# FoX attention by pairs of heads, with projections handed out in steps of three matmuls

## The reference

```python
q = rms_norm(q.reshape(b, t, FOX_HEADS, HEAD_DIM), q_norm)
k = rms_norm(k.reshape(b, t, FOX_HEADS, HEAD_DIM), k_norm)
cum_log_f = jnp.cumsum(jax.nn.log_sigmoid(f_logit), axis=1)
for start in range(0, t, FOX_BLOCK):          # FOX_BLOCK = 128
    end = start + FOX_BLOCK
    logits = jnp.einsum('bqhd,bkhd->bhqk', q[:, start:end], k[:, :end]) * scale
    logits = logits + cum_log_f[:, :, start:end, None] - cum_log_f[:, :, None, :end]
    probs = jax.nn.softmax(jnp.where(causal, logits, MASK_VALUE), axis=-1)
    outs.append(jnp.einsum('bhqk,bkhd->bqhd', probs, v[:, :end]))
o = rms_norm(jnp.concatenate(outs, axis=1), o_norm)
```

## Time and profile before

| | us |
|---|---|
| median of 3 runs | 1870.01 (1867.45 to 1887.97) |
| the profiled execution | 1867.99 |
| its span, first to last instruction | 1866.2 |
| TensorE matmul busy | 1731.4 (93%) |
| VectorE busy | 889.6 (48%) |
| ScalarE busy | 676.2 (36%) |

### The profile page before, as it was taken

One profiled execution on the slowest core, in us unless ns is written; L12 is line 12 of the kernel. 1 busy time (PEld: TensorE's weight loads), 2 busy tenths in 40 slices (PEclk: granted clock), 3 DMA queues, 4 the chain that ended last, 5 costly groups with the idle time before them and its releaser, 6 DMA issues.

```text
span 1866.2 us, 20863 instructions
## 1 busy us (share of the span) xinstructions
PE 1731.4 (93%) x8076; PEld 1374.7 (74%) x8076; DVE 889.6 (48%) x1487; ACT 676.2 (36%) x1218; POOL 74.2 (4%) x119
## 2 busy tenths in 40 slices
PE   6999998988888769699999999999999999999997
PEld 5787665655567546587888888888888888888886
DVE  4315584453636656545334434555543355555332
ACT  5224103633452353634434322434432334344321
POOL 2000430000001002000000000000000000000000
PEclk8999998898999899899999999999999999999999
DMA  4122000000002021350001102333323333433232
GB/s 138 45 47 46 13 12 12 23 12 12 12 23 68 12 68 57 111 194 11 14 1 46 45 29 87 94 102 91 96 74 96 101 113 98 123 92 107 85 96 96
DMA packets 166922, 121.32 MB, mean 65 GB/s; under 512 B 23448, under 2 KB 140456, under 8 KB 166824
## 3 DMA queue, kind: packets, MB, share of 16 engines
q1 hardware_dynamic: 165496, 115.53, 20.8%
q10 hardware_dynamic: 1328, 4.46, 0.7%
HBM read 115.77 MB, written 4.19 MB: 64 GB/s over the span
## 4 chain that ended last, share of the span: by engine, by line
PE 57%; DVE 1%; ACT 0%; DMA 0%; issue 0%; DVEq 0%
PE tail_b L99 17%; PE tail_b L101 17%; PE tail_b L100 17%; PE tail_b L2065 2%; PE tail_b L2040 1%; PE tail_b L2029 0%; PE tail_b L2052 0%; PE tail_b L1977 0%; DVE tail_wl L1741 0%; DMA tail_wr<-in_w_out 0%; PE tail_b L2184 0%; PE tail_b L2100 0%; DVE tail_xs L1776 0%; ACT tail_xs L1576 0%; DVE XR L1904 0%
## 5 line engine op out<-in xcount | busy, mean ns | idle before, releaser
L1897 DVE TENSOR_TENSOR ff_wl<-ff_wr,ff_wh 128x512 fp32r<-128x512 f32 (+1 forms) x176 | 168.5, 958 | 329.9 <-ACT ff_wh L1684 329.9
L1684 ACT ACTIVATE ff_wh<-ff_wr 128x512 fp32r<-128x512 f32 (+1 forms) x176 | 148.7, 846 | 377.9 <-PE tail_b L101 377.9
L99 PE MATMUL tail_b<-HH,ff_wh 128*128 128x512 f32 x704 | 273.9, 389 | 0.0
L100 PE MATMUL tail_b<-HL,ff_wh 128*128 128x512 f32 x704 | 273.9, 389 | 0.0
L101 PE MATMUL tail_b<-HH,ff_wl 128*128 128x512 f32 x704 | 273.9, 389 | 0.0
L99 PE MATMUL mix_gb<-HH,mix_wh 128*128 128x512 f32 x432 | 178.3, 413 | 7.7 <-ACT slots L444 3.8
L100 PE MATMUL mix_gb<-HL,mix_wh 128*128 128x512 f32 x432 | 171.5, 397 | 0.0
L101 PE MATMUL mix_gb<-HH,mix_wl 128*128 128x512 f32 x432 | 170.8, 395 | 0.0
L99 PE MATMUL tail_b<-tail_wh,HH 128*128 128x512 f32 x384 | 153.9, 401 | 10.0 <-DVE tail_wl L1741 8.8
L100 PEld LDWEIGHTS tail_b<-HL,ff_wh 128*128 128x128 f32 x704 | 132.2, 188 | 27.7
L99 PEld LDWEIGHTS tail_b<-HH,ff_wh 128*128 128x128 f32 x704 | 132.2, 188 | 27.5
(11 more groups left out here) (311 smaller groups left out, 2661.7 us busy)
## 6 DMA issues: line engine op xcount, KB each, us to landing
ff_wr<-in_ffn_w_up SPq DMA_DIRECT2D x88, 512.0 KB, 3.7
ff_wr<-in_ffn_w_down SPq DMA_DIRECT2D x88, 256.0 KB, 2.8
mix_wr<-in_w_in SPq DMA_DIRECT2D x26, 512.0 KB, 3.7
mix_wr<-in_xa_wkv SPq DMA_DIRECT2D x16, 512.0 KB, 3.7
XR<-in_x SPq DMA_DIRECT2D x8, 512.0 KB, 6.4
tail_wr<-in_w_out SPq DMA_DIRECT2D x16, 256.0 KB, 5.2
XR<-in_x ACTq DMA_DIRECT2D x1, 4096.0 KB, 18.7
tail_wr<-in_xa_wq SPq DMA_DIRECT2D x16, 256.0 KB, 4.6
```

What stands on the lines that cost most here:

```text
L99: pe.matmul(out, hi_w, hi_x, start=first, stop=False)
L100: pe.matmul(out, hi_w, lo_x, start=False, stop=False)
L1684: act.activation(part(FWH[m % FPART], m), part(FWR[m % FRAW], m), ACT.Copy).then_inc(w_hi, 1)
L1897: dve.tensor_tensor(part(FWL[m % FPART], m), part(FWR[m % FRAW], m), part(FWH[m % FPART], m), ALU.subtract)\
```

## The change

The 32 units become 16 pairs (`PAIRS`): both heads of `hp` for one block of queries. On TensorE, `scores(u, c)` issues piece c of the one head and then of the other, which use rows 0 to 63 and 64 to 127 of the array. `outputs(u)` goes over the key blocks and issues the value product of both heads for each; they write columns 0 to 63 and 64 to 127. `SC` has four buffers instead of three, `PTS` four, `CB` four, and the running sums of the second pair of heads are made among pairs 1 to 4 of the first.

VectorE scales no probabilities. The unscaled exponentials are transposed and multiplied with V; VectorE takes the reciprocals of both sums (`rin`), TensorE spreads each over 64 partitions by a matmul of the reciprocal column, broadcast, with the identity, and VectorE copies the result to `INV` and multiplies the output with it (`fox_out`, which ScalarE had before).

The projections in FoX go by steps, one step being the three matmuls of one k (`fill`). `FOX_PRE` has 6, 6, 5, 5, 5, 5 steps instead of six times 8, and every pair has two steps ahead of its later transposes (`FOX_A`) and two ahead of its outputs (`FOX_B`). ScalarE and VectorE do the copies and weight parts for a half in the round or pair in which it begins (`begun`), VectorE one pair later among the pairs.

```diff
-_FX = spread(2 * S0, 2 * G0, [1] * 6 + [1 if n in (4, 9, 14, 20, 25, 30) else 0 for n in range(33)])
-FOX_PRE, FOX_UNIT = _FX[:6], _FX[6:]
+def in_two(spans):
+    return spans[0::2], spans[1::2]
+def begun(span):
+    return -(-span[0] // KT), -(-span[1] // KT)
+_FX = spread(2 * S0 * KT, 2 * G0 * KT, [6, 6, 5, 5, 5, 5] + [2, 2] * 16)
+FOX_PRE, (FOX_A, FOX_B) = _FX[:6], in_two(_FX[6:])
...
+        PAIRS = [(hp, i) for hp in range(2) for i in range(NT)]
+        PIECES = [(u, c, hh) for u, (hp, i) in enumerate(PAIRS) for c in range(i // 4 + 1) for hh in range(2)]
...
ScalarE
+            def probs_out(u, g):
+                i = PAIRS[u][1]
+                w = len(blocks(i, g)) * P
+                for hh in range(2):
+                    m = group_of[(u, g, hh)]
+                    act.wait_ge(E("p_tr"), m + 1)
+                    if u >= 1:
+                        act.wait_ge(E("av_mm"), u)
+                    act.activation(PTS[2 * g + hh][:, 0:w], M[3 + m % 2][:, 0:w], ACT.Copy).then_inc(E("p_ev"), 1)
+            for u, (hp, i) in enumerate(PAIRS):
                 for g in range(i // 4 + 1):
+                    probs_out(u, g)
+                for entry in CUM_AT(u):
+                    cum_out(entry)
+                new = range(*begun((FOX_A[u][0], FOX_B[u][1])))
+                for m in new:
+                    copy_out(m)
+                if u + 1 < len(PAIRS):
+                    fox_exp(u + 1)
+                for m in new:
+                    halves(m, m + 1)
...
VectorE
-            def probabilities(n):
-                sc, keys = SC[n % 3], (FOX_UNITS[n][1] + 1) * P
-                dve.wait_ge(E("expd"), n + 1)
-                link(dve.reciprocal(RIN[:, n:n + 1], SUM[:, n:n + 1]))
-                dve.tensor_scalar(sc[:, 0:keys], sc[:, 0:keys], RIN[:, n:n + 1], None, ALU.mult).then_inc(E("probs"), 1)
+            def inverse_sums(u):
+                dve.wait_ge(E("expd"), 2 * u + 2)
+                dve.reciprocal(RIN[:, 2 * u:2 * u + 2], SUM[:, 2 * u:2 * u + 2]).then_inc(E("rin"), 1)
+            def fox_out(u):
+                hp, i = PAIRS[u]
+                dve.wait_ge(E("av_mm"), u + 1)
+                dve.tensor_copy(INV[:], M[5][:, P:2 * P]).then_inc(E("inv"), 1)
+                dve.wait_ge(E("inv"), u + 1)
+                dve.tensor_tensor(MX[:, hp, i * P:(i + 1) * P], M[5][:, 0:P], INV[:], ALU.mult).then_inc(E("av_ev"), 1)
+            logits(0)
+            maxima(0)
+            late = range(0)
+            for u in range(len(PAIRS)):
+                if u:
+                    fox_out(u - 1)
+                if u + 1 < len(PAIRS):
+                    logits(u + 1)
+                inverse_sums(u)
+                if u + 1 < len(PAIRS):
+                    maxima(u + 1)
+                for m in late:
+                    halves(m, m + 1)
+                late = range(*begun((FOX_A[u][0], FOX_B[u][1])))
...
TensorE
+            def outputs(u):
+                hp, i = PAIRS[u]
+                if u:
+                    pe.wait_ge(E("av_ev"), u)
+                pe.wait_ge(E("rin"), u + 1)
+                for hh in range(2):
+                    n = 2 * u + hh
+                    pe.matmul(M[5][64 * hh:64 * hh + 64, P:2 * P], RIN[:, n:n + 1].to_broadcast([P, 64]), ident,
+                              start=True, stop=True, skip_group_check=True)
+                for g in range(i // 4 + 1):
+                    pe.wait_ge(E("p_ev"), group_of[(u, g, 1)] + 1)
+                    for k in blocks(i, g):
+                        for hh in range(2):
+                            mm = pe.matmul(M[5][64 * hh:64 * hh + 64, 0:P],
+                                           VT[:, k, 128 * hp + 64 * hh:128 * hp + 64 * hh + 64],
+                                           PTS[2 * g + hh][:, (k % 4) * P:(k % 4 + 1) * P], start=(k == 0), stop=(k == i),
+                                           skip_group_check=True)
+                mm.then_inc(E("av_mm"), 1)
+            for entry in CUM(0):
+                cum_row(entry)
+            scores(0, 0)
+            for u, (hp, i) in enumerate(PAIRS):
+                new = u + 1 < len(PAIRS)
+                if new:
+                    scores(u + 1, 0)
+                if u == 0:
+                    fill(*FOX_A[u])
+                transposes(u, 0)
+                if new and PAIRS[u + 1][1] >= 4:
+                    scores(u + 1, 1)
+                if u:
+                    fill(*FOX_A[u])
+                if i >= 4:
+                    transposes(u, 1)
+                for entry in CUM_AT(u):
+                    cum_row(entry)
+                fill(*FOX_B[u])
+                outputs(u)
+            pe.wait_ge(E("av_ev"), len(PAIRS))
             norms(12, 16)
```

More of the change, by code:

```diff
@@ L622, in _, with cum_out @@
[L622 to L632, removed]
+            def cum_out(entry):
+                _, h, v = entry
+                m = group_of[entry]
+                if h >= 2:
+                    act.wait_ge(E("gated"), 2)
+                act.wait_ge(E("p_tr"), m + 1)
+                act.activation(half(CB[h], v), M[3 + m % 2][:], ACT.Copy).then_inc(E("p_ev"), 1)
@@ new lines, in maxima @@
+            def maxima(u):
+                i = PAIRS[u][1]
+                keys = (i + 1) * P
+                for hh in range(2):
+                    n, sc = 2 * u + hh, SC[2 * (u % 2) + hh]
+                    dve.wait_ge(E("sc_read"), piece_of[(u, i // 4, hh)] + 1)
+                    link(dve.tensor_tensor(sc[:, keys - P:keys], sc[:, keys - P:keys], NEGQ[:], ALU.add))
+                    dve.tensor_reduce(NM[:, n:n + 1], sc[:, 0:keys], AX.X, ALU.max, negate=True).then_inc(E("neg_max"), 1)
@@ L1231, in _, with transposes @@
-            pe.wait_ge(E("n_out"), 12)
-            for n in range(33):
-                if n % 16 == 0 and n < 32:
-                    if n:
-                        outputs(n - 1)
-                    cum_rows(n // 16)
-                    scores(n)
-                    scores(n + 1)
-                    continue
-                if n < 32 and (n + 1) % 16:
-                    scores(n + 1)
-                halves(*FOX_UNIT[n])
-                outputs(n - 1)
+            def transposes(u, g):
+                i = PAIRS[u][1]
+                for hh in range(2):
+                    m = group_of[(u, g, hh)]
+                    pe.wait_ge(E("expd"), 2 * u + hh + 1)
+                    pe.wait_ge(E("p_ev"), m - 1)
+                    for k in blocks(i, g):
+                        last = pe.transpose(M3[3 + m % 2][:, k % 4, :], SC[2 * (u % 2) + hh][:, k * P:(k + 1) * P], ident)
+                    last.then_inc(E("p_tr"), 1)
```

165 lines of the change are left out of this document (64 added, 101 removed).

## The result

The changed kernel takes 1806.34 us (median of 4, 1803.33 to 1807.4), the one before beside it 1868.77 (1867.45 to 1887.97). The ratio is 0.9646, with a 95% interval of 0.959 to 0.9703. I had said 1814 and 1802 to 1832; the kernel is 8 us better than that. The profiled executions took 1867.99 and 1803.33 us, 64.7 apart, against 54.5 forecast: some 10 us have to be found in my terms. The profiled execution is the fastest of the four; the kernel's second profile (experiment 8) took 1807.5, and where the two differ is said there.

What follows compares the result with a forecast made beforehand. TensorE was taken to bound every pair; its stretch terms, 118.1 us, became 124.2 with waits, clock and last output, against 168.3. That 44.1 plus 10.4 from the rounds, 54.5, off 1867.99 gave 1813.5, said as 1814; range 1802 to 1832.

Steps and rivals of the forecast that it cites:

- Both overlaps: Attention stretch: two heads' scores run side by side, halving 30.7 us of stream; value products likewise, halving 31.4.
- no rival: Rivals included: chain sets the pace, 1831, chance 0.13; one alternation doesn't overlap, 1829, chance 0.10; both fail, 1845, chance 0.02.
- the chain sets the pace: Rival: value products through exponentials bound each pair; exponentials 2 us late make pairs wait 1.1, so 1831; chance 0.13.
- 0.3 for entering and leaving each of 16 groups: Value products in the attention stretch: group cost added to 15.7 us of stream, making 20.5 us.
- My lower bound: Whole time 1802: group costs 0.1 instead of 0.3 (8 less), clock and chain costing nothing (3.5 less).
- I take 2.5: Attention stretch: 2.5 us allowed for a short spell at 1.2 GHz, between 0 and 10.
- 2.2 + 1.0: TensorE's waits in the stretch: about 2.2 us at the start for VectorE's gates, 1.0 where TensorE doesn't bound a pair.
- The last output costs 0.4 more: End of the attention stretch: 0.4 us added, as VectorE scales the last output.
- It is 1.3 more on 144: Value products: 1.3 us more if only the SSD rate of 0.135 per matmul holds.
- The clock at 10 and the start's wait doubled: Case for the forecast's own upper bound: low clock costing 10 us and the start's wait doubled, 1826.
- the doubled drains: Case for the upper bound: TensorE's tiling-change price of 0.2 to 0.3 per group doubled, about 12 us more, 1826.
- 1.5 after the pair's start: Pair of eight key blocks: second exponential's transposes come 1.5 us into the next pair, so the chain's period is 7.95.

Runs made afterwards that it cites:

- experiment 8: Changed kernel with seven projection steps moved from pairs with slack to the last norms: 1798.25 us; the unedited changed kernel, rerun beside it, 1807.17 us.
- 3: Changed kernel with both heads' score matmuls reading the first head's rows, 0 to 63: 1820.06 us, stretch 14.7 us more.
- 2: Changed kernel with both heads' value products in columns 0 to 63 from the second pair on: 1826.3 us, stretch 15.3 us more.
- 4: Kernel before, units by single heads, with only the projections changed to steps of three matmuls: 1844.65 us against 1867.78 us beside it.
- 7: Changed kernel with each row maximum issued twice on VectorE: 1813.72 us, stretch 6.6 us more.
- 6: Changed kernel with VectorE scaling the probabilities by the sums again before the transposes, without the small matmuls: 1806.9 us against 1807.17 us unedited.
- 5: Changed kernel with the projection steps as whole halves, eight together in every other pair: 1815.64 us.
- 1: Changed kernel with the second head's value products after all of the first head's: 1815.86 us, stretch 9.8 us more.

## Why the prediction was right, and where it was 10 us short

**The mechanisms held.** Both overlaps came as forecast: 15.4 and 15.7 were said, undoing them cost 14.7 (3) and 15.3 (2). The waits for ScalarE's copies went with the steps (4: 19.8 to 0.3), TensorE bounds the pairs (98% busy, three waits), and no rival showed. With 1.22 us more per head the chain costs only 6.6 (7), and the clock, far from staying down, is 1.00 throughout. That VectorE and ScalarE get less work was said to be worth nothing unless the chain sets the pace; in the longest pairs it would have (6), and what the sums on the outputs spare there about pays for their small matmuls. Part of the 10 us is luck of the execution: the second profile of the same kernel took 4.2 us more, with the same stretch of 116.2.

**The sizes that were off**, in the words of the working:
- "0.3 for entering and leaving each of 16 groups" of value products. I took a whole number of records at half price and the dearest change of shape that the rows show. Measured, it is about 0.1 a group (1.62 us for 28 records, of which 28 x 0.0546 is 1.53): 3.2 us of the 10. My lower bound had this case.
- Scores were 1.8 under, since a group leaves in 0.2 and enters in nothing that shows (1.06 for two 512-column slots of 0.427), where I had 0.3. The 24 groups of transposes were 0.9 under.
- "I take 2.5" for the clock: nothing. The spell of the earlier trace rows at 362 to 372 stood behind pairs where TensorE waited, and no pair waits now. 2.5 us. The second pair of heads, where the steps alone (4) still had a wait of 2.1 and 3.4 us of low clock behind it, has neither here.
- Waits, "2.2 + 1.0": 2.1. The start cost 1.3 + 0.8, and the 1.0 for places where the chain is late was not needed. 1.1 us.
- "The last output costs 0.4 more": it costs 1.5 less. I costed VectorE's two steps and not what ScalarE no longer does. ScalarE's timeline in the kernel before, then ScalarE's and VectorE's in the kernel after:

```profile
522.41 0.27 ACT L620 ACTIVATE XR<-mix_m 64x128 f32<-64x128 f32 x1 [1.62 <-PE mix_m L1227]
522.71 0.60 ACT L444 ACTIVATE slots<-mix_gb 128x512 f32<-128x512 f32 x1
523.32 1.28 ACT L635 ACT_TABLE_LOAD   x1
```

```profile
458.44 1.28 ACT L654 ACT_TABLE_LOAD   x1
```

```profile
459.94 0.29 DVE L917 COPY mix_bt<-mix_m 128x128 f32<-128x128 f32 x1 [6.10 <-PE mix_m L1271]
460.27 0.29 DVE L919 TENSOR_TENSOR XR<-mix_m,mix_bt 128x128 f32<-128x128 f32 x1
```

  The load of ScalarE's table of functions for the norms used to come behind its last output copy, at 523.32 in the kernel before, after the last value product. Now ScalarE has no outputs to copy and loads at 458.44, while TensorE is still in the value products (end 459.90). 1.9 us.
- Against these, projections with the running sums were 1.0 and the small matmuls 0.8 dearer: four records of a group take 398.14 to 398.41, 0.27, not 0.22.
- The rounds gave 0.65 more than said. I had taken 0.5 off for a round that ScalarE would hold up; TensorE shows 35.88 busy of 35.90. The time ahead of the rounds (+0.7) and behind the stretch (-0.6) cancel in this execution.

Together -3.2 - 1.8 - 0.9 - 2.5 - 1.1 - 1.9 - 0.65 + 1.8 is -10.3, against the 10.1 between 1813.5 and the profiled 1803.33 with its roundings.

**Slips in the working that the forecast didn't rest on.** "It is 1.3 more on 144" doesn't follow: 144 x 0.135 is 19.4, which is 3.7 over the bare 15.7 and 1.1 under the 20.5 with group costs. 64 steps of 3 x 0.2275 are 43.7, not 43.9. The clock at 10 and the start's wait doubled give 1823, and only the doubled drains give 1826. And "1.5 after the pair's start" is 0.9 where it matters (7): the pairs of eight blocks came nearer to waiting than the sum said, 0.6 us.

**Which part brought the gain.** The steps alone bring 23 us (4). Rows and columns overlapping bring some 14.7 and 15.3. What is left of the 62, about 9, wasn't tried by itself. I would put there the wait at the start of the second pair of heads that the steps alone leave (2 of 5.3), the two spells at 1.2 GHz behind those waits, fewer groups to enter and leave, and the table load, against 4.3 for the small matmuls; that is argued, not shown. Undone from the full version the steps cost only 9 (5), since in a pair the other head's work covers part of the copies: the parts share one pool of waiting, and their worths don't add.

The experiments' own misses have the same source. Where I charged a cost in every pair or in most of them (6, 7), it came only in the pairs whose slack was used up, and was about half of the sum.

## What to carry to other kernels

When 64-row or 64-column matmuls of two heads can alternate between halves of the array, count them at half price and 0.1 to 0.2 us per group, and look for enough small pieces of other work to put behind each transpose as well: done alone, that was the largest single part here (23 us), though it is worth only 9 once the heads are paired. A delay added to a chain costs only what exceeds the slack, so sum it over the units whose period is shorter than their chain, not over all. When an engine loses work, follow what it does next as well: here a table load moved out of the path, which was worth more than the step that I had costed. And before crediting an edit with a few us, compare the profiles from the last instruction that it can't have touched: 2 us of the 8.9 in experiment 8 lay ahead of it.

## What the runs showed of the hardware that I had not expected

- TensorE starts matmuls for a free column half ahead of earlier ones in the other half: 0.43 us ahead in 1, so that even the order by heads overlaps at each change, 2.77 us instead of 3.15 for 28 records.
- Two profiled executions of one program differ in the clock: 1.00 behind the last norms in one, 0.52 over 6 us in the other, with the same waits of 1.4, 1.1, 0.6 and 2.3 us ahead. That costs 2.8 us. Six of the eight profiles with these waits have it, none of the three with the waits filled. A stretch with the full clock in one profile is therefore no proof that its waits are cheap.
- In the alternating products 28 records of 128 columns take 1.62 us, 0.058 each, against 0.109 to 0.113 for one alone: the column halves overlap for nearly the whole factor of two, and the entry and exit of the group add only about 0.1.
